# An mLSTM and convolution decoder layer: the heads' gate items made by GpSimd instead of VectorE

## The reference, cut to what matters

```
log_i = ig;  log_f = log_sigmoid(fg)
bcum  = cumsum(log_f)                          (within a chunk)
m_t   = max(bcum + m, max_s(bcum_t - bcum_s + log_i_s))
w_intra = exp(bcum_t - bcum_s + log_i_s - m_t)
w_inter = exp(bcum + m - m_t)
w_s   = exp(bcum_end - bcum + log_i - m_new)   (weights of the new state)
decay = exp(bcum_end + m - m_new)              (decay of the old state)
```

## Time and profile before

| | |
|---|---|
| median of 3 runs | 950.72 us (950.71 to 952.53) |
| the profiled execution | 951.12 us, span 949.6 us |
| granted TensorE clock | 0.998 of full |
| PE busy | 926.8 us (98%) |
| DVE busy | 778.2 us (82%) |
| ACT busy | 463.7 us (49%) |
| POOL busy | 111.2 us (12%) |

### The profile page before, as it was taken

One profiled execution on the slowest core, in us unless ns is written; L12 is line 12 of the kernel. 1 busy time (PEld: TensorE's weight loads), 2 busy tenths in 40 slices (PEclk: granted clock), 3 DMA queues, 4 the chain that ended last, 5 costly groups with the idle time before them and its releaser, 6 DMA issues.

```text
span 949.6 us, 18383 instructions
## 1 busy us (share of the span) xinstructions
PE 926.8 (98%) x6801; PEld 904.0 (95%) x6801; DVE 778.2 (82%) x1238; ACT 463.7 (49%) x682; POOL 111.2 (12%) x113
## 2 busy tenths in 40 slices
PE   6999999999999999999999999999999999999996
PEld 5999999999999999999999999999999999999995
DVE  6899986898697969876445569999888999889996
ACT  5654452445245424634833345456445555556573
POOL 4111140042005100500221000000000000000001
PEclk9999999999999999999999999999999999999999
DMA  5245214311621262042342222232222223332122
GB/s 194 90 142 185 86 46 175 128 64 55 236 79 40 88 233 72 21 162 90 115 142 67 88 85 71 89 126 98 89 90 90 90 73 106 108 114 90 49 85 100
DMA packets 22371, 98.55 MB, mean 104 GB/s; under 512 B 2841, under 2 KB 5033, under 8 KB 17820
## 3 DMA queue, kind: packets, MB, share of 16 engines
q1 hardware_dynamic: 19504, 77.13, 24.4%
q0 software_dynamic: 1984, 19.71, 5.6%
q10 hardware_dynamic: 816, 0.88, 0.3%
HBM read 85.27 MB, written 12.44 MB: 103 GB/s over the span
## 4 chain that ended last, share of the span: by engine, by line
PE 81%; DVE 11%; issue 3%; ACT 2%; DMA 2%; POOL 0%; SPq 0%; POOLq 0%; DVEq 0%; ACTq 0%
PE ps L1288 43%; PE ps L1550 25%; PE ps L1523 3%; PE ps L1378 2%; PE ps L1402 2%; PE ps L1450 2%; DMA raw<-w_fp_in 1%; PE ps L1388 1%; DVE main L2161 1%; PE ps L1459 1%; DVE w_lo L1673 1%; PE ps L1435 1%; DVE hn L1733 1%; DMA raw<-w_cgcv_in 1%; DVE main L2181 1%
## 5 line engine op out<-in xcount | busy, mean ns | idle before, releaser
L1288 PE MATMUL ps<-h_hi,w_hi 128*128 128x288 f32 x896 | 194.0, 298 | 0.7 <-DVE w_lo L1673 0.7
L1288 PE MATMUL ps<-h_hi,w_lo 128*128 128x288 f32 x896 | 191.7, 296 | 0.0
L1288 PE MATMUL ps<-h_lo,w_hi 128*128 128x288 f32 x896 | 191.5, 296 | 0.0
L793 ACT ACTIVATE w_hi<-raw 128x1024 fp32r<-128x1024 f32 x76 | 80.3, 1056 | 177.1 <-PE ps L1288 174.4
L1288 PEld LDWEIGHTS ps<-h_hi,w_hi 128*128 128x128 f32 x896 | 143.3, 189 | 2.2 <-DVE w_lo L1673 0.9
L1288 PEld LDWEIGHTS ps<-h_hi,w_lo 128*128 128x128 f32 x896 | 144.2, 189 | 0.0
L1288 PEld LDWEIGHTS ps<-h_lo,w_hi 128*128 128x128 f32 x896 | 144.1, 189 | 0.0
L1673 DVE TENSOR_TENSOR w_lo<-raw,w_hi 128x1024 fp32r<-128x1024 f32 x76 | 93.5, 1231 | 49.6 <-ACT w_hi L793 49.5
L1901 DVE SCALAR_TENSOR_TENSOR conv<-a_p,vec,conv x120 | 97.7, 814 | 0.2
L1550 PE MATMUL ps<-cols_b,late 128*128 128x288 f32 x432 | 62.8, 295 | 0.0
L1550 PE MATMUL ps<-cols_a,main 128*128 128x288 f32 x432 | 62.8, 295 | 0.0
(11 more groups left out here) (358 smaller groups left out, 1863.8 us busy)
## 6 DMA issues: line engine op xcount, KB each, us to landing
raw<-w_head_in SPq DMA_DIRECT2D x40, 512.0 KB, 3.5
raw<-w_fp_in SPq DMA_DIRECT2D x18, 1024.0 KB, 4.8
cs<-st_c_in POOLq DMA_DIRECT2D x4, 2048.0 KB, 9.6
c_s_out<-cs POOLq DMA_DIRECT2D x4, 2048.0 KB, 7.6
raw<-w_fo_in SPq DMA_DIRECT2D x8, 1024.0 KB, 4.9
x<-xT_in SPq DMA_DIRECT2D x16, 288.0 KB, 4.1
raw<-w_cgcv_in SPq DMA_DIRECT2D x8, 512.0 KB, 4.4
raw<-w_ga_in SPq DMA_DIRECT2D x8, 512.0 KB, 3.5
```

Source lines behind the costliest of these rows:

```text
L793: act.activation(w_hi[:, s, :], raw[:, s, :], ACT.Copy).then_inc(hi_ready, 1)
L1288: last = pe.matmul(ps[:, 2 * s + b, 0:HALF], wt[:, w, k * P:k * P + P], src[:, k, b * HALF:b * HALF + HALF], start=(k == 0 and wt is w_hi ...
```

## The change

The 13 instructions that make the items (ten `tensor_scalar` on 4x128, two `tensor_tensor` on 4x64, one on 4x8) leave VectorE's list and stand in GpSimd's, behind the transfers of `nrow`, `m_p`, `negm` and `mend`. The last of them raises `exps_in`, as before. `rows`, `t8` and `mend` stay on VectorE, and `mrow_ready` now counts five instructions: `rows`, `mrow`, `nrow`, `t8`, `mend`. GpSimd issues the transfer of `mend` at `mrow_ready` 5 and no longer at `exps_in`.

```diff
@@ gpsimd
-            pool.wait_ge(mrow_ready, 2)
+            pool.wait_ge(mrow_ready, 3)
             pool.dma_start(nrow_d, nrow[:, :]).then_inc(negm_spread, 16)
             pool.dma_start(m_p, mrow[:, TP - 1:TP]).then_inc(out_stored, 16)
             pool.wait_ge(negm_spread, 16)
             pool.dma_start(negm[:, :, :], nrow_d.partition_broadcast(P)).then_inc(negm_spread, 16)
-            pool.wait_ge(exps_in, 1)
+            pool.wait_ge(mrow_ready, 5)
             pool.dma_start(m_s, mend[:, :]).then_inc(out_stored, 16)
+            for t in range(NB):
+                steps.settle()
+                for s in range(t + 1):
+                    src = item(I_G + s) if s == t else item(OFF[s, t])
+                    if t < NB - 1:
+                        steps.on(pool.tensor_scalar(item(OFF[s, t + 1]), src, total(t), None, ALU.add))
+                    else:
+                        steps.on(pool.tensor_scalar(item(I_WS + s), src, total(t), mrow[:, TP - 1:TP],
+                                                   ALU.add, ALU.subtract))
+            steps.on(pool.tensor_tensor(per_sample(rows[:, I_WS * P + TP:I_WS * P + T]), per_sample(rows[:, TP:T]),
+                                       spread(t8[:, :]), ALU.add))
+            steps.on(pool.tensor_tensor(per_sample(rows[:, I_WI * P:I_WI * P + TS]), per_sample(nrow[:, TP:T]),
+                                       spread(m0[:, :]), ALU.add))
+            steps.settle()
+            pool.tensor_tensor(t8[:, :], t8[:, :], m0[:, :], ALU.add).then_inc(exps_in, 1)
             pool.wait_ge(exps_out, 4)
@@ scalar
-            act.wait_ge(mrow_ready, 1)
+            act.wait_ge(mrow_ready, 2)
@@ vector
-            steps.on(dve.tensor_tensor(rows[:, 0:T], li[:, :], ft[:, :], ALU.subtract))
+            dve.tensor_tensor(rows[:, 0:T], li[:, :], ft[:, :], ALU.subtract).then_inc(mrow_ready, 1)
             dve.tensor_tensor_scan(mrow[:, :], lfm[:, :], lim[:, :], 0.0, ALU.add, ALU.max).then_inc(mrow_ready, 1)
-            dve.wait_ge(mrow_ready, 1)
+            dve.wait_ge(mrow_ready, 2)
             end = slice(TP + SL - 1, T, SL)
             dve.tensor_tensor(nrow[:, :], ft[:, :], mrow[:, :], ALU.subtract).then_inc(mrow_ready, 1)
-            steps.on(dve.tensor_tensor(t8[:, :], ft[:, end], mrow[:, end], ALU.subtract))
-            steps.on(dve.tensor_copy(mend[:, :], mrow[:, end]))
-            (the same 13 instructions on dve, with scaled(3) and split_lo(5, 1) after the first of them)
+            dve.tensor_tensor(t8[:, :], ft[:, end], mrow[:, end], ALU.subtract).then_inc(mrow_ready, 1)
+            dve.tensor_copy(mend[:, :], mrow[:, end]).then_inc(mrow_ready, 1)
+            scaled(3)
+            split_lo(5, 1)
             conv_input(1)
             scaled(4)
             split_lo(6, 0)
```

More of the change, by code:

```diff
@@ L697, in _, with total, item, per_sample @@
             pool.dma_start(negm[:, :, :], nrow_d.partition_broadcast(P)).then_inc(negm_spread, 16)
-            pool.wait_ge(exps_in, 1)
+            pool.wait_ge(mrow_ready, 5)
             pool.dma_start(m_s, mend[:, :]).then_inc(out_stored, 16)
+            def total(t):
+                return ft[:, t * P + P - 1:t * P + P]
+            def item(n):
+                return rows[:, n * P:n * P + P]
+            for t in range(NB):
[7 more added lines that the diff above has]
+                                                   ALU.add, ALU.subtract))
+            def per_sample(t):
+                return t.rearrange("p (b j) -> p b j", b=SB)
+            def spread(t):
+                return t.unsqueeze(2).broadcast_to([NH, SB, SL])
+            steps.on(pool.tensor_tensor(per_sample(rows[:, I_WS * P + TP:I_WS * P + T]), per_sample(rows[:, TP:T]),
[4 more added lines that the diff above has]
+            pool.tensor_tensor(t8[:, :], t8[:, :], m0[:, :], ALU.add).then_inc(exps_in, 1)
             pool.wait_ge(exps_out, 4)
@@ L1829, in _ @@
-            steps.settle()
-            dve.tensor_tensor(t8[:, :], t8[:, :], m0[:, :], ALU.add).then_inc(exps_in, 1)
+            dve.tensor_tensor(t8[:, :], ft[:, end], mrow[:, end], ALU.subtract).then_inc(mrow_ready, 1)
+            dve.tensor_copy(mend[:, :], mrow[:, end]).then_inc(mrow_ready, 1)
+            scaled(3)
+            split_lo(5, 1)
             conv_input(1)
```

## The result

| | before | after |
|---|---|---|
| median of 6 runs each, same chip | 951.05 us (950.69 to 952.53) | 959.12 us (958.11 to 959.9) |
| the profiled execution | 951.12, span 949.6 | 959.21, span 957.7 |
| granted TensorE clock | 0.998 | 0.994 |

What follows compares the result with a forecast made beforehand. TensorE, 98% busy, was taken as the bound, except up to 77.6 us where VectorE's list sets the time. Signal 51.97 + 3.7 + 2.6 = 58.3, less 53.76, gives 4.5 us: 951.12 + 4.5 = 955.6, median 955.2, range 952.4 to 958.8.

Steps and rivals of the forecast that it cites:

- the stretch in which the time is set: Up to 77.6 us VectorE's list sets the time, ending where TensorE's unit 9 waited 0.69 us for w_lo.
- the freed 2.8 us: VectorE's estimated saving from losing the 13 instructions; it turns into waiting before normalised_lo(0), worth at most unit 9's 0.7 us.
- the hour E of the signal: When GpSimd raises exps_in, letting ScalarE start the exponentials: 53.27 us before, forecast 58.3 us.
- E less 53.76: Loss rule: any signal after 53.76 us shifts the VectorE and ScalarE pattern up to unit 9 rigidly; forecast loss 4.5 us.
- the start at 52.0: GpSimd's first item begins at 51.97 us, right after issuing the transfer of mend.
- rival b: GpSimd's transfers hold its arithmetic until negm lands at 57.6 us: loss 7.5 us, time 958.2, chance 0.09.
- When GpSimd raises E: Step timing GpSimd's 13 instructions at 0.29 us an item after 51.97; alone, signal at 55.7 us and loss 1.9 us.
- The term of 3.7 us: GpSimd's 13 instructions alone: twelve at 0.29 us and 0.2 for the last, overlap and waits roughly cancelling.
- the likely upper end, 0.44: Upper price in us of one GpSimd item, from a two-input addition over 288 columns cut to 128, setup kept.
- rival (d): A tensor_scalar on GpSimd takes 0.79 us like that addition: loss 11 us, time 961.7, chance 0.04.
- The second term: From 52.70 us GpSimd's items alternate with VectorE's split_lo(6) and two hn, each waiting for the other: GpSimd held 2.6 us.
- The path at unit 9: TensorE would stand 3.9 us before unit 7 and about 1.3 before unit 9, instead of 0 and 0.7.

Runs made afterwards that it cites:

- experiments 1 and 6: 1: kernel before, ScalarE held by eight unread GpSimd fills, 958.78 us for 951.04. 6: changed kernel without the 13 instructions, signal at once, 949.85 for 951.24.
- experiment 7: Changed kernel with GpSimd making the items before its transfers of nrow, m_p, negm and mend: 958.32 us for 951.24, ratio 1.0071.
- experiment 5: Changed kernel with h_hi of rows 0 to 3 and w_hi of unit 7 before ScalarE's wait, items turned at unit 7's last block: 955.87 us for 951.24.
- experiment 8: Changed kernel with VectorE making the first six sums and GpSimd only the last seven instructions: 956.24 us for 951.24, ratio 1.0049.
- experiment 3: Changed kernel with 46 unused matmuls in TensorE's wait before unit 7: 959.22 us for 951.04; with w_lo of unit 9 also moved ahead, 958.70 (958.99 without matmuls) for 951.51.
- experiment 2: Kernel before, VectorE still making the items, ScalarE held by four unread GpSimd fills instead of eight: 954.75 us for 951.04, ratio 1.0048.

## Why the prediction was wrong in size, and how far its mechanism held

Right: the stretch in which the time is set; that the freed 2.8 us turn into waiting (VectorE idles 9.29 us ahead of `h_lo` of row 0; experiments 1 and 6); that the loss goes by the hour E of the signal and is near E less 53.76 (table above); the start at 52.0 (52.16); that the transfers in flight hold no arithmetic (rival b; its 958.2 came near the measured time by another road).

The step that failed is "When GpSimd raises E": "I take 0.29, the row nearest in shape". The term of 3.7 us for the 13 instructions measured 7.7.

| | forecast | measured |
|---|---|---|
| start of the first item | 51.97 | 52.16 |
| the 13 instructions alone | 3.7 | 7.7, worked out (6 x 0.60, 4 x 0.78, 0.28, 0.29, 0.19, and small gaps) |
| contention | 2.6 | 1.5 (the rest of the 9.2) |
| E | 58.3 | 61.3 |
| loss, by E - 53.76 | 4.5 | 7.6 |
| loss, medians | | 8.1 |

The items' price was short by 4.0 us in sum; with a start 0.2 later and 1.1 less contention that makes the 3.0 by which E was missed. The last 0.5 us, from 7.6 to 8.1, lie within the interval. It also fell outside what I called the likely upper end, 0.44; rival (d), with 0.79 for every item, had the true price for the four with two scalars and was too high for the six with one, and I gave it 0.04 as "only its size speaks for it". That was the wrong way to weigh it: no row was a tensor_scalar, so nothing but size spoke for 0.29 either. VectorE's own 0.27 and the copy's 1 ns a column said nothing about arithmetic on GpSimd; the only arithmetic row, 0.79 for 288 columns, is 2.7 ns a column, and taken per column without a setup it gives 0.35, about half of what was measured.

The second term was wrong in kind. "They alternate, one instruction each, and each waits for the whole of the other's" doesn't hold for these small items: GpSimd did nearly all the waiting. In narrow windows of the changed kernel:

```profile
52.16 0.60 POOL L712 TENSOR_SCALAR rows<-rows,ft 4x128 f32<-4x128 f32 x1
52.86 1.63 POOL L712 TENSOR_SCALAR rows<-rows,ft 4x128 f32<-4x128 f32 x1
...
52.87 1.23 DVE L1702 TENSOR_TENSOR w_lo<-raw,w_hi 128x1024 fp32r<-128x1024 f32 x1 [0.40 <-ACT w_hi L822]
...
54.02 0.84 DVE L1762 SCALAR_TENSOR_TENSOR hn<-x,vec,rs 128x576 f32<-128x576 f32 x1
...
54.47 0.86 POOL L712 TENSOR_SCALAR rows<-rows,ft 4x128 f32<-4x128 f32 x1
```

The item at 52.86 overlapped `w_lo` and ended behind it (54.49 for 54.10), 1.0 us longer than its neighbour, while `w_lo` kept its 1.23 and the two `hn` took 1.68 for 1.54. How much it costs GpSimd grows with VectorE's two-input work beside it: 1.5 us here, 3.8 in experiment 7 (11.5 less 7.7), 5.7 in experiment 5. With a larger GpSimd instruction VectorE does wait, as the tap of the earlier trace rows did, 1.79 us for 0.75. The Trainium skill ("SBUF — State Buffer", section "Who interferes with whom") has such pairs exclude each other, whoever comes first getting the ports; the first half agrees with these rows, the second doesn't: in experiment 8 an item stood 3.17 us while VectorE's instructions followed one another.

The Trainium skill ("GPSIMD Engine Reference", section "Engine selection") puts two-input elementwise work on GpSimd at about twice VectorE's time and one-input work at roughly line rate. The shortest copy, 0.29, is near VectorE's times for this shape, but tensor_scalar isn't: 0.60 and 0.78 for VectorE's 0.27 and 0.33.

The path at unit 9 wasn't the forecast one either. The prediction had TensorE wait 1.3 us there for `w_lo`; it didn't wait at all, since two things moved that the prediction had put at nothing: unit 7 took 2.4 us more at the fallen clock, and `w_lo` of 9 was only 6.7 us late, with GpSimd's fill off the copies. TensorE stood 6.7 and not 3.9 us before unit 7, the clock fell behind that, and unit 9 began 8.5 us later by TensorE's own delay. That the end is again near E - 53.76 is in part luck: from 8.5 at unit 9 the delay goes to 7.6 at the first attention and to 8.1 at the end, and what takes it down and up again wasn't followed.

What the fallen clock costs by itself is settled only in part. `w_lo` of 9 was there at 84.34 and unit 9 began at 86.17, so it can have cost up to 1.8 us there. With the clock kept (experiment 3) the copies took their longer time again and unit 9 began 0.7 us earlier, and the median didn't move (959.22 for 959.12).

## What to carry to other kernels

Work moved to an idle engine costs its latency there, not its load: find who waits for its last signal, and what else stands in that waiter's list. Here 13 small instructions held four `h_hi` and one `w_hi` on ScalarE, and through them TensorE. Where the trace has no row of the very operation on the very engine, the price is unknown by a factor of two or three, and a row of another operation with the same shape doesn't narrow it. Look at the one wait that the profile names before unloading an engine: putting `w_lo` of unit 9 ahead of work with slack gained 1.3 us (0.3 to 2.0) with no instruction moved between engines. And taking work out from behind a late signal helps only down to the next thing that still stands behind it, as `h_hi` of row 4 did in experiment 5.

## What was not expected of the hardware

- tensor_scalar on GpSimd over 4x128: 0.52 us with an immediate, 0.60 with one scalar column, 0.78 with two and a second operation; the shortest copy 0.29. VectorE's tensor_scalar takes 0.27 with one column and 0.33 with two.
- Between small tensor_scalar on GpSimd and long two-input work on VectorE the contention is nearly one-sided: 13 instructions of 7.7 us alone took 9.2, 11.5 and 13.4 beside more and more of that work, whose `w_lo` stayed at 1.22 to 1.30 us.
- A fill on GpSimd (128x2176, 1.92 us) and three copies of 32x4 on VectorE: 2.72 us for the copies where the fill ran beside them, 0.54 where it came behind.
- In experiment 2 the clock showed 1.00 through TensorE's wait and fell only after it had started again at 67.16 (0.90 from 67 to 69, 0.50 from 69 to 71).
- Arithmetic on GpSimd started 0.04 us after its own issue of a transfer (51.60 + 0.52 to 52.16), with a 1152 KB transfer on its way, issued at 51.04 and landed 6.9 us later.
